# Norm, turn and routing of each 128-token tile inside the mixer's last part

## The reference

```python
for i in range(DEPTH):
    j = i // N_MIXERS
    if i % N_MIXERS == 0:
        y = _gated_deltanet_mixer(...)
    else:
        y = _mla_mixer(...)
    x = _layernorm(DEEPNORM_ALPHA * x + y.astype(x.dtype), ln1_g[i], ln1_b[i])
    y = _grouped_moe(x, router_w, router_bias, moe_w_gate[i], moe_w_up[i], moe_w_down[i])
    x = _layernorm(DEEPNORM_ALPHA * x + y.astype(x.dtype), ln2_g[i], ln2_b[i])
...
scores = jax.nn.sigmoid((t @ router_w).astype(jnp.float32))
```

## Time and profile before

| | us |
|---|---|
| median of 3 runs | 1866.23 |
| lowest, highest | 1861.76, 1868.33 |
| the profiled execution | 1864.28 |
| its span, first to last instruction | 1862.5 |
| mean granted clock of TensorE | 0.922 of full |

### The profile page before, as it was taken

One profiled execution on the slowest core, in us unless ns is written; L12 is line 12 of the kernel. 1 busy time (PEld: TensorE's weight loads), 2 busy tenths in 40 slices (PEclk: granted clock), 3 DMA queues, 4 the chain that ended last, 5 costly groups with the idle time before them and its releaser, 6 DMA issues. The chain is left out here.

```text
span 1862.5 us, 20168 instructions
## 1 busy us (share of the span) xinstructions
PE 1580.2 (85%) x6814; PEld 990.2 (53%) x6814; DVE 878.0 (47%) x1786; ACT 326.6 (18%) x737; POOL 159.3 (9%) x143
## 2 busy tenths in 40 slices
PE   7894999999999999999887399973899997389990
PEld 4473576585765857658585244432555553334440
DVE  3562564665656656566564311116145456311115
ACT  2120122121221212212121011101222221011110
POOL 1200200202002020020200100002000000100002
PEclk9997999999999999999996599996899998599995
DMA  5782110101101011000104489945021112669964
GB/s 184 221 270 76 45 45 23 45 23 45 45 23 45 23 45 45 23 23 0 46 1 153 167 270 354 352 157 175 0 81 36 46 34 73 235 208 351 355 233 144
DMA packets 150500, 219.69 MB, mean 118 GB/s; under 512 B 8584, under 2 KB 120448, under 8 KB 150464
## 3 DMA queue, kind: packets, MB, share of 16 engines
q1 hardware_dynamic: 138464, 176.50, 29.6%
q10 hardware_dynamic: 7392, 25.96, 4.0%
q0 software_dynamic: 4608, 16.78, 2.5%
HBM read 175.70 MB, written 43.52 MB: 118 GB/s over the span
## 5 line engine op out<-in xcount | busy, mean ns | idle before, releaser
L1395 PE MATMUL bank<-moe_wgu,moe_xgT 128*96 128x512 f32 x512 | 228.0, 598 | 1.5 <-DVE moe_xgT L1602 1.5
L404 PE MATMUL bank<-xT,wqkv 128*128 128x512 f32 x448 | 211.0, 601 | 9.6 <-DVE conv L896 9.6
L1395 PEld LDWEIGHTS bank<-moe_wgu,moe_xgT 128*96 128x96 f32 x512 | 81.9, 165 | 123.2 <-issue 123.2
L1602 DVE COPY moe_xgT<-bank 128x384 f32<-128x384 f32 x34 | 19.0, 558 | 226.5 <-PE bank L1386 226.5
L488 PE MATMUL bank<-wz,xT 128*128 128x256 f32 x512 | 118.3, 381 | 0.9 <-DVE res L1089 0.9
L404 PEld LDWEIGHTS bank<-xT,wqkv 128*128 128x128 f32 x448 | 78.1, 191 | 74.3 <-issue 63.6
L1412 PE MATMUL bank<-moe_wd,moe_hidT 128*96 128x512 f32 x256 | 115.2, 593 | 1.8 <-DVE moe_hidT L1610 1.8
L620 PE MATMUL bank<-wo,oT 128*128 128x512 f32 x256 | 115.7, 602 | 0.8 <-ACT oT L772 0.8
L488 PEld LDWEIGHTS bank<-wz,xT 128*128 128x128 f32 x512 | 96.3, 191 | 14.2 <-issue 1.7
L896 DVE SCALAR_TENSOR_TENSOR conv<-bank,taps,conv 128x510 f32<-128x510 f32 (+1 forms) x128 | 95.2, 744 | 0.6
L987 DVE TENSOR_TENSOR TU<-TU,bank 128x512 f32<-128x512 f32 x112 | 75.7, 686 | 16.2 <-PE bank L547 7.3
(11 more groups left out here) (297 smaller groups left out, 2445.1 us busy)
## 6 DMA issues: line engine op xcount, KB each, us to landing
moe_wgu<-moe_w_gate SPq DMA_DIRECT2D x32, 1024.0 KB, 10.5
moe_wgu<-moe_w_up SPq DMA_DIRECT2D x32, 1024.0 KB, 13.0
moe_wd<-moe_w_down SPq DMA_DIRECT2D x32, 1024.0 KB, 6.2
wqkv<-dn_w_in SPq DMA_DIRECT2D x32, 512.0 KB, 4.0
moe_x_rows<-slots_x ACTq DMA_DIRECT2D x34, 384.0 KB, 7.3
slots_y<-moe_y_rows ACTq DMA_DIRECT2D x32, 384.0 KB, 6.0
slots_x<-o SPq DMA_DIRECT2D x1, 9984.0 KB, 51.2
slots_y<-o SPq DMA_DIRECT2D x1, 9984.0 KB, 92.6
```

What stands on the lines that cost most here:

```text
L404: mm = pe.matmul(bank[:], wqkv[:, ct, k], xT[:, k], start=k == 0, stop=k == KD - 1)
L1395: mm = pe.matmul(ps[2][0:CAP], xgT[:, r, k], wgu[:, r, k].rearrange("p a f -> p (a f)"), start=k == 0, stop=k == KD - 1)
```

## The change

The norm, the turn and the routing of a tile move from `route_and_run` into the last part of the mixer ahead of it, in both layers. A new class `Arrival` holds them. DVE takes the statistics of a tile when both its halves are added, aggregates them and negates the mean (`spread`), and makes the two passes over the tile before it (`apply`). POOL makes the deviation of each tile by itself (8 instructions in place of 2). PE turns and routes in the same order as before, into banks 4 to 6 and 7 in place of 0 to 3 and 4; in layer 0 the turn of tile 0 stands behind the projection piece 5, ahead of pieces 6 and 7, and in layer 1 behind piece 7. ACT's copies and its exponential come behind its last work in the mixer; the exponential goes to a buffer that outlives the phase. `RowNorm` stays for the norm behind the experts. The diff, cut:

```diff
...
+        rows = Arrival(nc, t, sb, sem, 0)
...
@@ -623,6 +624,13 @@
                         turn_kq(uses, i, i + 1)
                     if with_next and n == 5:
                         scores(uses, i, i + 1)
+                    if not with_next and n == 5:
+                        rows.turn(pe, 0)
+                if not with_next:
+                    for tt in range(1, TT):
+                        rows.turn(pe, tt)
+                        rows.route(pe, tt - 1)
+                    rows.route(pe, TT - 1)
 
             pe.wait_ge(taps_ready, 1)
             pe.wait_ge(dve_sums, 1)
@@ -787,6 +795,7 @@
             with act.Fori(0, NK - 1) as i:
                 body(i, MAIN, True)
             body(NK - 1, LAST, False)
+            rows.on_scalar(act)
 
         @block.gpsimd
         def _(pool):
@@ -825,6 +834,7 @@
             with pool.Fori(0, NK - 1) as i:
                 body(i, True)
             body(NK - 1, False)
+            rows.on_gpsimd(pool)
 
         @block.vector
         def _(dve):
@@ -1089,12 +1099,13 @@
                     nc.vector.tensor_tensor(y, y, bank[:], ALU.add).then_inc(y_ready, 1)
                     if with_next and n == 5:
                         mask_scores(uses, i, i + 1)
-                    if not with_next:
-                        if n:
-                            row_stats(nc, t, n - 1)
+                    if not with_next and half:
                         dve.wait_ge(y_ready, 1 + i * 8 + n + 1)
+                        rows.spread(dve, tt)
+                        if tt:
+                            rows.apply(dve, tt - 1)
                 if not with_next:
-                    row_stats(nc, t, 7)
+                    rows.apply(dve, TT - 1)
                 if with_next:
                     assert links["k"] == per, links["k"]
 
...
+class Arrival:
+
+
+    def __init__(self, nc, t, sb, sem, which):
+        self.nc, self.t, self.which = nc, t, which
+        self.g, self.b = t["gains"][:, which % 2, 0], t["gains"][:, which % 2, 1]
+        self.mv, self.rstd, self.neg = sb("row_mv", [P, TT, 2]), sb("row_rstd", [P, TT]), sb("row_neg", [P, TT])
+        self.stats_ready, self.spread_ready, self.rstd_added, self.rstd_ready, self.centred, self.normed, self.turned, self.xT_ready, self.logits = (
+            sem(n) for n in ("stats_ready", "spread_ready", "rstd_added", "rstd_ready", "centred", "normed", "turned", "xT_ready_again", "logits"))
+
+    def spread(self, dve, tt):
+        for half in range(2):
+            row_stats(self.nc, self.t, 2 * tt + half).then_inc(self.stats_ready, 1)
+        dve.wait_ge(self.stats_ready, 2 * tt + 2)
+        self.nc.vector.bn_aggr(self.mv[:, tt], self.t["stats"][:, tt].rearrange("p h s -> p (h s)")).then_inc(self.spread_ready, 1)
+        dve.wait_ge(self.spread_ready, tt + 1)
+        self.nc.vector.tensor_scalar(self.neg[:, tt:tt + 1], self.mv[:, tt, 0:1], -1.0, None, ALU.mult).then_inc(self.centred, 1)
+
+    def apply(self, dve, tt):
+        rows = self.t["res"][:, tt]
+        if tt == 0:
+            dve.wait_ge(self.t["gain_in"][self.which], 32)
+        dve.wait_ge(self.centred, 2 * tt + 1 + (tt < TT - 1))
+        self.nc.vector.scalar_tensor_tensor(out=rows, in0=rows, scalar=self.neg[:, tt:tt + 1], in1=self.g, op0=ALU.add, op1=ALU.mult).then_inc(self.centred, 1)
+        dve.wait_ge(self.centred, 2 * tt + 2 + (tt < TT - 1))
+        dve.wait_ge(self.rstd_ready, tt + 1)
+        self.nc.vector.scalar_tensor_tensor(out=rows, in0=rows, scalar=self.rstd[:, tt:tt + 1], in1=self.b, op0=ALU.mult, op1=ALU.add).then_inc(self.normed, 1)
+
+    def on_gpsimd(self, pool):
+        for tt in range(TT):
+            pool.wait_ge(self.spread_ready, tt + 1)
+            rsqrt(self.nc, self.t, pool, self.rstd[:, tt:tt + 1], self.mv[:, tt, 1:2], C_EPS_LN, self.rstd_added, tt + 1).then_inc(self.rstd_ready, 1)
+
+    def turn(self, pe, tt):
+        ps, ident = self.t["ps"], self.t["const"][:, C_ID:C_ID + P]
+        pe.wait_ge(self.normed, tt + 1)
+        for half in range(2):
+            n = 2 * tt + half
+            if n >= 3:
+                pe.wait_ge(self.xT_ready, n - 2)
+            for k in range(4):
+                mm = pe.transpose(ps[4 + n % 3][:, k * P:(k + 1) * P], self.t["res"][:, tt, (half * 4 + k) * P:(half * 4 + k + 1) * P], ident)
+            mm.then_inc(self.turned, 1)
+
+    def route(self, pe, tt):
+        if tt == 0:
+            pe.wait_ge(self.t["router_in"], 32)
+        pe.wait_ge(self.xT_ready, 2 * tt + 2)
+        for k in range(KD):
+            mm = pe.matmul(self.t["ps"][7][:, tt * NE:(tt + 1) * NE], self.t["xT"][:, k, tt * P:(tt + 1) * P], self.t["router_w"][:, k], start=k == 0, stop=k == KD - 1)
+        if tt == TT - 1:
+            mm.then_inc(self.logits, 1)
+
+    def on_scalar(self, act):
+        for n in range(8):
+            tt, half = n // 2, n % 2
+            act.wait_ge(self.turned, n + 1)
+            act.copy(self.t["xT"][:, half * 4:half * 4 + 4, tt * P:(tt + 1) * P], self.t["ps"][4 + n % 3][:].rearrange("p (k n) -> p k n", k=4)).then_inc(self.xT_ready, 1)
+        act.wait_ge(self.logits, 1)
+        act.activation(self.t["gate_exp"][:].rearrange("p t e -> p (t e)"), self.t["ps"][7][:, 0:TT * NE], ACT.Exp, scale=-1.0)
+
+
...
@@ -1279,9 +1352,8 @@
             return ctx.enter_context(nc.sbuf_tensor(f"{name}_{n}", shape, dt))
 
         sem = phase(nc, ctx, name + "_")
-        rows = RowNorm(nc, t, sb, sem, which)
-        rw, rb = t["router_w"], t["router_b"]
-        s, sel, decay, w = (sb(n, [P, TT, NE]) for n in ("s", "sel", "decay", "w"))
+        rb, decay = t["router_b"], t["gate_exp"]
+        s, sel, w = (sb(n, [P, TT, NE]) for n in ("s", "sel", "w"))
         counted = sb("counted", [P, TT + 1, NE])
         chosen = counted[:, 0:TT]
         beat, tie = sb("beat", [P, 16, 4, 4]), sb("tie", [P, 16, 4, 4])
@@ -1293,7 +1365,7 @@
         slot2 = sb("slot2", [P, 2, TT])
         owner_f = sb("owner_f", [P, EXTRA])
 
-        turned, xT_ready, logits, e_ready, link = (sem(n) for n in ("turned", "xT_ready", "logits", "e_ready", "link"))
+        link = sem("link")
         chosen_ready, ranked, place_ready, scattered = (sem(n) for n in ("chosen_ready", "ranked", "place_ready", "scattered"))
         gu_in, d_in = [sem(f"gu_in{n}") for n in range(RING)], [sem(f"d_in{n}") for n in range(RING)]
         rows_loaded, stored = [sem(f"rows_loaded{n}") for n in range(3)], [sem(f"stored{n}") for n in range(3)]
@@ -1336,7 +1408,6 @@
 
         @block.gpsimd
         def _(pool):
-            rows.on_gpsimd(pool)
             pool.wait_ge(place_ready, 1)
             for k in range(2):
                 for tt in range(TT):
@@ -1345,30 +1416,6 @@
 
         @block.tensor
         def _(pe):
-            def turn(tt):
-
-                rows.wait(pe, tt)
-                for half in range(2):
-                    n = tt * 2 + half
-                    if n >= 4:
-                        pe.wait_ge(xT_ready, n - 3)
-                    for k in range(4):
-                        mm = pe.transpose(ps[n % 4][:, k * P:(k + 1) * P], res[:, tt, (half * 4 + k) * P:(half * 4 + k + 1) * P], ident)
-                    mm.then_inc(turned, 1)
-
-            def route(tt):
-                pe.wait_ge(xT_ready, 2 * tt + 2)
-                for k in range(KD):
-                    mm = pe.matmul(ps[4][:, tt * NE:(tt + 1) * NE], xT[:, k, tt * P:(tt + 1) * P], rw[:, k], start=k == 0, stop=k == KD - 1)
-                return mm
-
-            turn(0)
-            pe.wait_ge(t["router_in"], 32)
-            for tt in range(1, TT):
-                turn(tt)
-                route(tt - 1)
-            route(TT - 1).then_inc(logits, 1)
-
             pe.wait_ge(chosen_ready, 1)
             pe.matmul(ps[5][:, 0:80], before, counted[:].rearrange("p t e -> p (t e)"), start=True, stop=False)
             for tt in range(TT):
@@ -1432,12 +1479,6 @@
 
         @block.scalar
         def _(act):
-            for n in range(8):
-                tt, half = n // 2, n % 2
-                act.wait_ge(turned, n + 1)
-                act.copy(xT[:, half * 4:half * 4 + 4, tt * P:(tt + 1) * P], ps[n % 4][:].rearrange("p (k n) -> p k n", k=4)).then_inc(xT_ready, 1)
-            act.wait_ge(logits, 1)
-            act.activation(decay[:].rearrange("p t e -> p (t e)"), ps[4][:, 0:64], ACT.Exp, scale=-1.0).then_inc(e_ready, 1)
             act.wait_ge(scattered, 16 * 2 * TT)
 
             def load_rows(e, r):
@@ -1502,8 +1543,6 @@
         def _(dve):
             step = Steps(dve, link)
             nc.vector.memset(counted[:, TT], 0.0)
-            rows.on_vector(dve, step)
-            dve.wait_ge(e_ready, 1)
             dve.wait_ge(t["router_in"], 32)
             step(nc.vector.tensor_scalar(decay[:], decay[:], 1.0, None, ALU.add))
             step(nc.vector.reciprocal(s[:], decay[:]))
@@ -1592,8 +1631,6 @@
             nc.vector.tensor_copy(counts[:], ends[0:1, NE - 1:NE])
 
```

(14 more changed lines are left out.)

## The result

The changed kernel takes 1876.84 us (median of 9 runs, 1870.93 to 1881.44), the kernel before, measured beside it, 1866.23 (9 runs, 1861.76 to 1870.19). The ratio is 1.0053, with a 95% interval of 1.0039 to 1.0068: slower by 10 us. The time lies inside the range of 1859 to 1877, 0.16 us from its end, outside the forecast's own range of 1866.5 to 1873.5, and 7.3 us above the forecast of 1869.5. The profiled execution took 1876.84, which is 12.56 more than that of before; its span is 1875.0, 12.5 more.

The account below looks back on a forecast made before the run. Work ahead of the first expert counts in full in both layers, with PE's turns and routes ending the first stretch. Lost 9.2 less won 5.95 gave +3.25 us, forecast 1869.5 against a median of 1866.23; range 1859 to 1877.

Parts of the forecast that it names:

- the forecast's own range: Range of the favoured case, low clock in the routing chain and packets taking turns: 1866.5 to 1873.5 us, chance 0.66.
- Part 1: Norm, turn and routing moved into the mixer's last part: arithmetic starts 4.35 us earlier in layer 0, 1.6 in layer 1.
- the case of 1871.4: Layer 0: clock falls during PE's 1.7 us wait, projections 6 and 7 take twice as long, holding DVE 1.9 us.
- Part 2: Scatter and first row load meet weights still in flight, packets alternating one for one: 4.6 us lost in each layer.
- even bytes: At the scatter, both queues share bytes evenly, so it ends as late as the weights: 11.0 us lost a layer.
- the second rival: At the scatter, bytes are shared evenly or all weights go ahead: +16.05 us, 1882.3, chance 0.14.
- weights first: At the scatter, all 3.9 MB of remaining weights go ahead of it: 11.0 us lost a layer.
- the upper bound of 11.0: Most the scatter could lose per layer: 3.9 MB of weights at 354 GB/s, 11.0 us.
- step 2: Signs of the scatter's loss: DMA share above 0.9 throughout, q0 with three quarters of the time in its second half.
- The 34: Forecast distance from first weight issue to last scatter landing: some 34 us, not 30.
- the clock rival: PE's clock holds through turns and routes, chain ends at 1018.2 and 1591.2: 19.15 us won, 1856.3, chance 0.10.

## Why the prediction missed the size

**Part 1, the move, was right.** The forecast had the arithmetic start at 1024.8 in layer 0, won 4.35: 1024.97, won 4.15. Layer 1, won 1.6: 1.40. Sum 5.95, measured 5.55. Its steps held too: tile passes 5.5 apart (5.6), projections 6 and 7 at the upper level behind tile 0's turn (3.60 us for 8; the case of 1871.4 didn't occur), the clock at 0.50 from 1009 on, PE as the bound from the third tile on (1009.79 to 1023.42, 13.63 us, forecast 13.8), POOL's power hidden (on one column a tile it took 0.55 to 1.56 us, less than the 2.03 of the earlier trace rows). What bounds the stage was read rightly: a stage of 26 us taken away gives back only what its last wait gives back.

**Part 2, the mechanism was right**: the weights lose their cover and meet the scatter. It was the larger part, and of the right sign. Once both flow, packets take turns one for one, as the earlier trace rows had it; the even bytes of the second rival are refuted (360 and 358 packets, 78.9 and 25.2% of the time). But the other half of its name, weights first, is in part what happened: 1.7 MB went ahead of the scatter, and nearly all that was left ahead of the rows. That all engines' transfers run on the same 16 and interleave, as the Trainium skill says (DMA: Bandwidth & Descriptors, Issuing engines are not separate DMA queues), agrees: in the middle of the scatter the two shares add up to 104%. Its section Queues, rings and completion order says that an engine turns between the queues it has work for at each packet; by that alone q0's first packet would have come within a few packets of the 1.84 us it needs alone, and the trace has 4.56. Either the work had not reached the engines, or the turn isn't taken: that stays open.

**The step that failed is the sum of part 2**, "190 x 10.1 = 1.9 us, the other 834 one of 1 KB each, 834 x 2.9 = 2.4, and the first load of gathered rows, 96 packets, 0.3. Sum 4.6 us lost in each layer":

- *The scatter, 4.3 counted, 4.54 and 5.03 measured*: right in sum, wrong in its parts. 2.72 and 2.83 of it are the delay ahead of the first packet, which the sum didn't have. The flow from first packet to last grew by only 1.84 and 2.06. The 1.9 against 4-KB packets fell away because of that delay: by q0's first packet q1 had moved some 6.6 MB (4.83 in the first 15.1 us, 1.72 in the next 4.5), and the six loads ahead of expert 2 are 6.3 MB. The q1 packets that then met the scatter, 1341 of 1.37 MB, took 3.9 us of the 16 engines, and about half of that cost nothing: alone the scatter filled 92.5% of their time (1048 to 1052, before), beside weights the two add up to 104%.
- *The first rows, 0.3 counted, 4.66 and 3.16 measured*: here the forecast was lost, by 7.2 us in both layers. I priced the 96 packets, not the time until the last of 16 engines had done its share. It is the delay ahead of the first packet again (2.89 and 2.87 after the load's issue, not 1.05 and 0.99, with 1.19 and 1.20 MB of weights moved meanwhile), and engines that don't finish together: before, the 16 finished the first load between 1061.0 and 1061.6; in the changed kernel between 1063.4 and 1066.6, twelve by 1064.4 and one each at 1064.9, 1065.4, 1065.9 and 1066.6. The turn waits for the last.
- *The first product, 0 counted, 0.82 and 1.11 measured*: the clock's level at its start. I had written that all behind the passage is unmoved. Over the runs this product takes 8.47 to 10.10, so that this loss comes from the change isn't shown.

Predicted +3.25, with part 1's 0.4 less, the scatter's 1.0 more, the rows' 7.2 and the product's 1.9 more and the 1.3 given back: +12.4, and the spans differ by 12.5. From issue to turn the layers lost 9.20 and 8.19, below the upper bound of 11.0; but I had given the upper end to even bytes alone, a mechanism that isn't there. That the time still lies in the range is luck: the range reached up to 1877 for even bytes. And the signs of step 2 came true (share above 0.9, first weight issue to last landing 33.6 us for 34, three quarters of the time for q0) without seeing the miss. The 34 was itself a hint: its terms, 15, 10 to 12 and 4.6, add up to 30 to 32, and what they leave out is the 1.84 us from the scatter's issue to its first packet, the term that grew. The earlier trace rows show a queue in mid-flow beside another; they can't tell what a queue pays to start there, nor when its last engine is done, and I took them for both. Two figures of the forecast were also off without moving the sum: expert 2's gate and up landed 36.3 us after the phase's start and not some 26, still 31 us ahead of their use, and the clock rival's 1018.2 and 1591.2 come out of its terms as 1018.0 and 1591.1.

## What to carry to other kernels

Before a stage is taken apart to overlap its work, ask what its transfers hid behind it, and move them too, or hold back those that aren't needed at once: here 4.2 MB held behind one wait turned 1.0053 into 0.9971. A chain of small transfers that wait for one another (scatter, then rows, then PE) is dear beside bulk loads. Price it, in each link of the chain, by what is still open on the other queue when it is issued and by when the slowest of the 16 engines ends, and not by its packets. When PE waits for data anyway, a couple of idle matmuls of 512 columns at the end of that wait can buy the clock's upper level for what follows: here 7.08 us in place of 8.83 and 9.47, in one profiled execution.

## What the runs showed of the hardware

- A queue that gets its first work while another has the engines full: first packet 3.3 to 5.0 us after the issue, mostly 4.4 and more (GpSimd's indirect DMA), 1.7 to 1.8 alone; 2.1 to 3.4 (the activation engine's load) against 1.0. The wait goes with the weights issued before it: 1.67 to 1.78 MB of them moved first where 2.6 to 3.6 MB were open, 1.14 of 1.21 and 1.50 of 1.66 MB where little was. 1-KB packets alone, or half-sized loads, didn't shorten it (4.99 and 4.64 in layer 0).
- Under such a load the 16 engines drift apart: their ends of one load lay 0.6 us apart before and 3.2 after in layer 0, 0.7 and 1.7 in layer 1. The three row loads of the changed kernel took 8.1, 8.7 and 9.2 us from issue to landing in layer 0 (minimum, median, maximum), 3.5, 4.5 and 5.3 before.
- Before the change PE's level fell while it was idle (0.85 from 1004 to 1006, no matmul) and then stayed at 0.50 though turns and matmuls of 16 columns kept it busy for 20.57 of 26 us. In the changed kernel it was 0.50 from 1015 to 1017, and with idle matmuls of 448 columns in between 1.00, both with 2.00 of 2 us busy. The Trainium skill (TensorE: Matmul & The Clock Gate, What's actually happening) lets the level follow how busy the array has lately been. These rows have both levels at equal busy time, and in layer 1 the filled chain fell once and held once, so an engine's busy time in the profile doesn't foretell its level.
- The ninth load's issue, at 1042.62, held SP for 11.74 us, and that load landed 24.2 us after it. Of the eight loads ahead of it four had landed (the fourth at 1040.15) and the fifth landed at 1043.13. Before the change the ninth issue held SP for 3.58 us, with no scatter beside it.
